# Expert weights in 4 MB transfers, and the order of scatter, gather, last expert and final norm changed

## The reference

```python
gu = xb @ w1[ex] + b1[ex]                 # w1: 1024 x 2048 for each of 32 experts
gate = jnp.minimum(gu[:, :D_FF_EXPERT], SWIGLU_LIMIT)
up = jnp.clip(gu[:, D_FF_EXPERT:], -SWIGLU_LIMIT, SWIGLU_LIMIT)
glu = gate * jax.nn.sigmoid(gate * SWIGLU_ALPHA)
return ((up + 1.0) * glu) @ w2[ex] + b2[ex]   # w2: 1024 x 1024
...
contrib = yb * row_w[:, None]             # weighted by the router's share, summed per token
...
return rmsnorm(x, final_g)
```

## Time and profile before

| | before |
|---|---|
| time, median of 3 runs | 1141.22 us (1140.94 to 1141.25) |
| the profiled execution: its own time | 1141.12 us |
| the profiled execution: its span, first to last instruction | 1139.3 us |
| PE busy | 1078.2 us, 95% of the span |
| DVE busy | 285.8 us, 25% |
| ACT busy | 102.2 us, 9% |
| read from memory | 434.98 MB, 383 GB/s over the span |
| 2 MB transfers | 192, each 40.7 us (median) from issue to landing |

### The profile page before, as it was taken

How to read it: one execution, slowest core, us unless ns; L and a number is a source line. 1 busy time by engine, 2 the same in 40 slices (tenths; PEclk the granted TensorE clock), 3 DMA queues, 4 the chain that set the end, 5 groups by cost and what they waited for, 6 DMA issues and landing times.

```text
span 1139.3 us, 13050 instructions
## 1 busy us (share of the span) xinstructions
PE 1078.2 (95%) x5177; PEld 474.2 (42%) x5177; DVE 285.8 (25%) x614; ACT 102.2 (9%) x215; POOL 11.2 (1%) x20
## 2 busy tenths in 40 slices
PE   7999999899999999999999999999999999999996
PEld 6788788733333333333333333333233323333332
DVE  4652422322222222222222222221211112222222
ACT  1121430200000000000000000000000000000001
POOL 1100000000000000000000000000000000000000
PEclk9999999999999999999999999999999999999999
DMA  9963158589999999999999999999999999999994
GB/s 364 370 258 123 60 224 349 203 350 399 427 429 427 430 427 429 429 427 430 427 430 427 430 427 429 429 427 430 427 429 428 430 427 429 429 427 430 427 430 193
DMA packets 35378, 436.31 MB, mean 383 GB/s; under 512 B 5312, under 2 KB 5696, under 8 KB 7488
## 3 DMA queue, kind: packets, MB, share of 16 engines
q1 hardware_dynamic: 34640, 435.63, 91.3%
q10 hardware_dynamic: 720, 0.42, 0.1%
HBM read 434.98 MB, written 1.05 MB: 383 GB/s over the span
## 4 chain that ended last, share of the span: by engine, by line
PE 71%; DMA 18%; SPq 6%; DVE 4%; issue 1%; ACT 0%; another core or an unknown queue 0%; POOL 0%; DVEq 0%; POOLq 0%; ACTq 0%
PE bank L762 27%; DMA ring<-in_w 17%; PE bank L791 15%; PE bank L490 8%; SPq L342 5%; PE bank L729 4%; PE bank L679 4%; PE bank L685 3%; PE bank L604 2%; PE bank L586 2%; DVE work L1118 1%; PE bank L747 1%; PE bank L525 1%; PE bank L539 1%; DMA ring<-in_w_in 1%; PE bank L510 1%
## 5 line engine op out<-in xcount | busy, mean ns | idle before, releaser
L762 PE MATMUL bank<-ring,work 128*64 128x512 f32 x2048 | 451.1, 593 | 22.6 <-DMA ring<-in_w 21.8
L762 PEld LDWEIGHTS bank<-ring,work 128*64 128x64 f32 x2048 | 144.4, 137 | 309.4 <-issue 259.1
L791 PE MATMUL bank<-ring,work 128*64 128x512 f32 x1024 | 235.5, 602 | 18.1 <-DVE work L1118 18.1
L791 PEld LDWEIGHTS bank<-ring,work 128*64 128x64 f32 x1024 | 68.2, 137 | 142.0 <-issue 116.3
L1109 DVE TENSOR_SCALAR work<-bank 128x512 f32<-128x512 f32 x32 | 22.1, 692 | 418.0 <-PE bank L762 418.0
L490 PE MATMUL bank<-ring 128*128 128x256 f32 x432 | 96.5, 381 | 0.0
L1228 ACT ACTIVATE work<-work 128x512 f32<-128x512 f32 x32 | 20.1, 629 | 758.4 <-DVE work L1109 758.4
L490 PEld LDWEIGHTS bank<-ring 128*128 128x128 f32 x432 | 81.1, 190 | 13.2 <-issue 2.4
L679 PE MATMUL bank<-x2n,work 128*64 128x512 f32 x264 | 63.9, 604 | 0.8 <-DVE work L1024 0.8
L729 PE MATMUL bank<-work 64*128 64x512 f32 x256 | 63.6, 615 | 0.9 <-DVE work L1122 0.9
L1044 DVE TENSOR_TENSOR work<-bank,vec 128x256 f32<-128x256 f32 x66 | 25.0, 420 | 141.2 <-PE bank L685 141.2
(11 more groups left out here) (174 smaller groups left out, 441.6 us busy)
## 6 DMA issues: line engine op xcount, KB each, us to landing
ring<-in_w SPq DMA_DIRECT2D x192, 2048.0 KB, 40.7
ring<-in_w_in SPq DMA_DIRECT2D x16, 1024.0 KB, 17.5
ring<-in_w_out SPq DMA_DIRECT2D x4, 1024.0 KB, 4.7
ring<-in_w_up_a SPq DMA_DIRECT2D x2, 1024.0 KB, 12.2
ring<-in_w_up_b SPq DMA_DIRECT2D x2, 1024.0 KB, 7.6
ring<-in_na_rpb SPq DMA_DIRECT2D x1, 1536.0 KB, 18.4
out<-x2n SPq DMA_DIRECT2D x4, 256.0 KB, 2.1
ring<-in_consts SPq DMA_DIRECT2D x1, 864.0 KB, 13.3
```

The costliest lines, as they stand in the source:

```text
L762: last = pe.matmul(bank[CAP * a:CAP * (a + 1), bk, :], kT, pairs[:, pair_of(par, k // 2), at + q * 512:at + (q + 1) * 512], start=False, s ...
L791: last = pe.matmul(bank[CAP * a:CAP * (a + 1), BH, :], fT, pairs[:, pair_of(par, c), at + a * 512:at + (a + 1) * 512], start=f == 0, stop= ...
```

## The change

It has these parts.

1. Transfers. The weights of the experts are laid out so that two neighbouring chunks form one run of 32 KB per partition. Experts 4 to 29 ("quads") are loaded with three transfers of 4 MB each instead of six of 2 MB, each waiting until PE has used both chunks that it replaces. Experts 0 to 3 and 30 stay at 2 MB. In expert 31 the last w1 chunk comes in two pieces and the last w2 chunk in three.
2. Alignment. Chunk 0 moves to slot 12, chunks 1 to 24 to slots 0 to 11, twice around, and odd experts use pairs 0 to 5 in order. Four of the early 2 MB loads of expert 1 wait for one chunk less than before, and expert 1's second one is issued ahead of the wait for the attention's end.
3. PE's order within an expert. `scatter()` and `gather()` no longer follow the w1 matmuls: the scatter comes at k == 4, the gather at k == 6. After the last w1 matmul the next thing in PE's stream is the wait for `hid_ready`. The wait for `xgT_ready` is split in two halves. In the last expert `turn_gathered` is left out.
4. The b1 split. Its transfers no longer wait for `scale_done`, four of its six steps on DVE move to c == 3, two stay at c == 4. The router's weights are laid out for one contiguous run per partition, and ACT squares x ahead of issuing three small transfers.
5. The final norm. ACT sums the squares in halves of 512, DVE multiplies by final_g meanwhile, and the scaling by the norm's factor is shared by DVE and ACT, each with its own store.

The core of the diff:

```diff
+            def load_quad(blk, q, par, used):
+                w, at = (w1, q) if q < W1_CH // 2 else (w2, 0)
+                first = pair_of(par, 2 * q)
+                sp.wait_ge(chunk_used, used)
+                sp.dma_start(pairs[:, first:first + 2, :].rearrange("p s n -> p (s n)"),
+                             w[bass.ds(blk, 1), at].rearrange("e p n -> p (e n)")).then_inc(quad_landed[par][q], 16)
...
-            with sp.Fori(1, E // 2) as j:
+            with sp.Fori(2, E // 2 - 1) as j:
                 for par in range(2):
-                    for c in range(BLK):
-                        load_chunk(2 * j + par, c, par, (2 * j + par - 2) * BLK + (PRE + c + 1))
+                    for q in range(BLK // 2):
+                        load_quad(2 * j + par, q, par, (2 * j + par - 2) * BLK + (PRE + 2 * q + 2))
...
                 for k in range(D // P):
-                    if k % 2 == 0:
+                    if k % 4 == 0:
+                        pe.wait_ge(xgT_ready, 2 * b + (k // 4 + 1))
+                    if last_one and k // 2 == 3:
+                        pe.wait_ge(piece_landed[k - 6], 16)
+                    elif quads:
+                        if k % 4 == 0:
+                            pe.wait_ge(quad_landed[par][k // 4], landings)
+                    elif k % 2 == 0:
                         pe.wait_ge(pair_landed[par][k // 2], landings)
+                    if k == 4 and not first:
+                        pe.wait_ge(down_ready, b)
+                        scatter()
+                    if k == 6:
+                        pe.wait_ge(pick_ready, b + 2)
+                        gather()
...
-                if not first:
-                    pe.wait_ge(down_ready, b)
-                    scatter()
-                pe.wait_ge(pick_ready, b + 2)
-                gather()
                 pe.wait_ge(hid_ready, b + 1)
                 turn(BH, lambda j: hid[:, j * P:(j + 1) * P], 4, hidT_done)
...
-                    if f == TURN_F:
+                    if f == TURN_F and not last_one:
...
-                if c == 4:
+                if c == 3:
                     dve.wait_ge(b1_landed, 16 * PARTS)
...
+                if c == 4:
                     ch.link(dve.tensor_tensor(b1_raw[low, :], b1_raw[low, :], b1_parts[low, :], ALU.subtract))
...
+                    act.activation(junk[:, 2 * m + a, :], bank[:, BY + 2 * m + a, :], ACT.Square, scale=D ** -0.5,
+                                   accum_out=ssq[:, a, m:m + 1]).then_inc(square_act, 1)
...
+                act.activation(x2n[:, m, 512:D], x2n[:, m, 512:D], ACT.Identity, scale=rstd[:, 2, m:m + 1]).then_inc(act_out, 1)
```

More of the change, by code:

```diff
@@ L245, in build_block @@
         b1_split = sem("b1_split")
-        landed = [sem(f"chunk_landed{n}") for n in range(SLOTS)]
+        landed = [sem(f"chunk_landed{n}") for n in range(SLOTS + 1)]
         pair_landed = [[sem(f"pair_landed{par}_{c}") for c in range(W1_CH + W2_CH)] for par in range(2)]
@@ L269, in build_block @@
         scatT_done, scatT_ready, down_ready, scatter_done = sem("scatT_done"), sem("scatT_ready"), sem("down_ready"), sem("scatter_done")
+        piece_landed = [sem(f"last_piece_landed{n}") for n in range(5)]
+        z_done, square_act, act_out = sem("z_done"), sem("square_act"), sem("act_out")
         y_done, out_ready, out_stored = sem("y_done"), sem("out_ready"), sem("out_stored")
@@ L278, in slot_of @@
         def slot_of(chunk):
-            return chunk % SLOTS
+            return (chunk - 1) % SLOTS if chunk else SLOTS
         def landings(chunk):
-            return 16 * (chunk // SLOTS + 1)
+            return 16 * ((chunk - 1) // SLOTS + 1) if chunk else 16
+        quad_landed = [[sem(f"quad_landed{par}_{q}") for q in range((W1_CH + W2_CH) // 2)] for par in range(2)]
+        LAST_CUTS = {3: [(0, slice(0, 2048)), (1, slice(2048, 4096))],
+                     5: [(2, slice(0, 2048)), (3, slice(2048, 3072)), (4, slice(3072, 4096))]}
         def pair_of(par, c):
-            return (c + 1) % BLK if par else BLK + c
+            return c if par else BLK + c
         BLK = W1_CH + W2_CH
@@ L327, in _ @@
                 sp.dma_start(xT[:, ks, :], xT_in[:, ks, :]).then_inc(xT_landed[n], 16)
-                sp.dma_start(ring[:, 0, cols], w_in[0][:, cols]).then_inc(first_landed[n] if n < 2 else landed[0], 16)
+                sp.dma_start(ring[:, SLOTS, cols], w_in[0][:, cols]).then_inc(first_landed[n] if n < 2 else landed[SLOTS], 16)
             def chunk_source(n):
@@ L382, in _ @@
             load_chunk(0, 5, 0, PRE)
[L383 removed]
+            for par in range(2):
+                for c in range(BLK):
+                    load_chunk(2 + par, c, par, par * BLK + PRE + c + 1)
+            with sp.Fori(2, E // 2 - 1) as j:
                 for par in range(2):
[L385 to L386 removed]
+                    for q in range(BLK // 2):
+                        load_quad(2 * j + par, q, par, (2 * j + par - 2) * BLK + (PRE + 2 * q + 2))
+            for c in range(BLK):
+                load_chunk(E - 2, c, 0, (E - 4) * BLK + PRE + c + 1)
+            for c in range(BLK):
+                if c not in LAST_CUTS:
+                    load_chunk(E - 1, c, 1, (E - 3) * BLK + PRE + c + 1)
+                    continue
+                sp.wait_ge(chunk_used, (E - 3) * BLK + PRE + c + 1)
+                for n, cols in LAST_CUTS[c]:
+                    sp.dma_start(pairs[:, pair_of(1, c), cols], pair_source(E - 1, c, cols)).then_inc(piece_landed[n], 16)
             sp.wait_ge(chunk_used, PRE + (E - 1) * BLK + 1)
@@ L399, in _ @@
             for m in range(MT):
[L400 to L403, removed]
+                sp.wait_ge(out_ready, m + 1)
+                sp.dma_start(out[0, m * P:(m + 1) * P, 0:512], x2n[:, m, 0:512]).then_inc(out_stored, 16)
             sp.wait_ge(out_stored, 2 * 16 * MT)
@@ L436, in project_first @@
             def project_first():
-                w = ring[:, 0, :].rearrange("p (k n) -> p k n", n=CW)
+                w = ring[:, SLOTS, :].rearrange("p (k n) -> p k n", n=CW)
                 for n, ks in enumerate(FIRST):
-                    pe.wait_ge(first_landed[n] if n < 2 else landed[0], 16)
+                    pe.wait_ge(first_landed[n] if n < 2 else landed[SLOTS], 16)
                     for a in range(2):
@@ L807, in _ @@
             expert_block(1, 1, 16)
-            with pe.Fori(1, E // 2) as j:
+            for par in range(2):
+                expert_block(2 + par, par, 32)
+            with pe.Fori(2, E // 2 - 1) as j:
                 for par in range(2):
-                    expert_block(2 * j + par, par, j * 16 + 16)
+                    expert_block(2 * j + par, par, (j - 1) * 16, quads=True)
+            expert_block(E - 2, 0, 48)
+            expert_block(E - 1, 1, 48, last_one=True)
             n_over = pe.value_load(ctrl[0:1, OVER:OVER + 1], min_val=0, max_val=OVER_MAX)
             with pe.If(n_over > 0):
+                pe.wait_ge(xg_ready, E + 1)
+                turn_gathered()
                 with pe.Fori(0, OVER_MAX) as j:
                     with pe.If(j < n_over):
-                        expert_block(j + E, 0, j * 16 + 16 * (E // 2 + 1))
+                        expert_block(j + E, 0, j * 16 + 64)
                     pe.nop()
@@ L1135, in _, with weigh, mean_square, scale_out @@
             dve.wait_ge(final_g_landed, 16)
-            for m in range(MT):
[L1137 to L1144, removed]
+            def weigh(m, a):
+                return dve.tensor_tensor(x2n[:, m, a * 512:(a + 1) * 512], bank[:, BY + 2 * m + a, :],
+                                         gf_b[:, a * 512:(a + 1) * 512], ALU.mult)
+            def mean_square(m):
+                dve.wait_ge(square_act, 2 * m + 2)
+                dve.tensor_scalar(msq[:, 2, m:m + 1], ssq[:, 0, m:m + 1], ssq[:, 1, m:m + 1], EPS,
+                                  ALU.add, ALU.add).then_inc(msq_ready, 1)
+            def scale_out(m):
+                dve.wait_ge(rstd_ready, 3 + m)
+                dve.wait_ge(z_done, 2 * m + 2)
+                dve.tensor_scalar(x2n[:, m, 0:512], x2n[:, m, 0:512], rstd[:, 2, m:m + 1], None,
+                                  ALU.mult).then_inc(out_ready, 1)
+            for m in range(MT):
+                dve.wait_ge(y_done, m + 1)
+                weigh(m, 1).then_inc(z_done, 1)
+                dve.wait_ge(square_act, 2 * m + 1)
+                weigh(m, 0).then_inc(z_done, 1)
+                if m == 0:
+                    mean_square(0)
+            scale_out(0)
+            mean_square(1)
+            scale_out(1)
         @block.scalar
@@ L1150, in _ @@
             act.dma_start(C("ident"), consts[:, CONST["ident"]]).then_inc(ident_landed, 16)
+            for n, ks in enumerate(FIRST):
+                act.wait_ge(xT_landed[n], 16)
+                act.activation(square[:, ks, :], xT[:, ks, :], ACT.Square).then_inc(square_done, 1)
```

(12 more changed lines are left out.)

65 lines of the change are left out of this document (35 added, 30 removed).

## The result

The changed kernel takes 1261.55 us (median of 4 runs, 1259.63 to 1263.71) against 1141.24 before, a ratio of 1.105 (95% interval 1.103 to 1.107). It is slower by 120 us. The prediction had the sign and the order of size, and it named the two things that cost the time.

A forecast was written before the change was run, and what follows sets the result against it. Transfers bound the kernel before, PE after, at 30.06 us per expert. 225.77 + 33.74 + 931.86 less 0.6, + 9.1 + 1.82 gave 1201.7; clock falls of 21.7 made 1223 us, range 1196 to 1257.

The forecast's parts named there:

- What bounds the kernel: Per expert before the change: transfers set the pace at 29.37 us, PE needs 27.15, leaving PE 2.2 us of slack.
- The bare chain: From last w1 matmul to the turns: PE waits uncovered for DVE's hidden values, 2.91 us in every expert.
- the spacing without clock falls: From one expert's b1 product to the next: 27.15 + 2.91 = 30.06 us at the high clock.
- the rival without falls: PE's clock never falls in the expert loop: 1202 us in all, chance 0.11.
- the price of a fall: Low PE clock after the gap before the turns: 0.7 us per expert, bounds 0 and 1.77.
- a full fall in each expert: Each of 31 experts pays 1.77 us for low clock: 1256.6 us or a little more, chance 0.11.
- start of expert 0's w1: Early part up to expert 0's w1: 228.35 less 2.58 for the b1 split's wait, 225.77 us.
- expert 0, to the next b1 product: From expert 0's w1 start to the next b1 product: 1.87 us longer than before, 33.74 us.
- 31 experts, to w2's end: 31 experts of 30.06 us, less 0.6 for the last one's saved turns, plus 21.7 for clock falls.
- end: From w2's end to the span's end: 10.1 us before, some 1.0 less after (bounds 0 and 2), 9.1.
- outside the span: Part of the execution's time not inside the profiled span: 1.82 us, as before the change.
- The rival on the other side: Transfers stay the bound if PE's period is below 29.2 us per expert: faster, about 1135 us, chance 0.06.

The follow-up runs named there:

- a_fill6: Changed kernel plus 6 needless gather-shaped products per expert except the first, between the last w1 matmul and the hid_ready wait: 1206.57 us, ratio 1.058.
- b_order_only: Kernel before the change with only the scatter moved to k == 4 and the gather to k == 6: 1263.6 us, ratio 1.106.
- a_scatter_back: Changed kernel with the scatter alone put back behind the w1 matmuls, the gather still at k == 6: 1142.24 us, ratio 0.9997.

## Why the prediction was right and wrong

**What bounds the kernel.** The reading of the pace held: PE 27.15 by itself, the transfers 29.37, PE the bound after the change. The bare chain was forecast at 2.91, and the wait in it measured at 2.86; the spacing without clock falls was forecast at 30.06 and measured at 30.08 (a_fill6). The forecast of the rival without falls, 1202, stands against 1205.54 for the profiled execution of that kernel; of the difference 2.5 us are in the early part and 0.7 in the end (both below).

**The clock.** This is the step that failed: the price of a fall, taken as 0.7 us per expert between bounds of 0 and 1.77. It measured 1.8 (1.78 against the measured 30.08, 1.80 against 30.06), two and a half times the forecast and at the upper bound. I argued that a low stretch beginning inside the gap spends half of itself on no work, and that not every expert need have one. In the trace each of experts 1 to 31 has one, and they start late: in expert 3 the clock falls as the turns begin, so that a stretch of 3.4 us costs 1.21 to 1.44 and not 0.9. And in each third expert the low stretch is twice as long (6.8 us against 3.4, by the windows above) and costs 2.68. The single fall in the earlier trace rows was the price of one stretch of 3.4 us and no bound on what an expert can lose. What came was my rival "a full fall in each expert", 1256.6 and "a little more if the low level should last longer", to which I had given 0.11.

The range ended at 1257, which is that rival without the little more. With the clock at its bound, it was the early part (3.8 us late in sum) and the end (0.7) that carried the time over the edge.

**The sum, term by term**, against the profiled execution. The forecast sum is 1223.4.

| term | forecast | measured | difference |
|---|---|---|---|
| start of expert 0's w1 | 225.77 | 231.55 | +5.8 |
| expert 0, to the next b1 product | 33.74 | 263.27 - 231.55 = 31.72 | -2.0 |
| 31 experts, to w2's end | 931.3 + 21.7 | 1251.29 - 263.27 = 988.0 | +35.0 |
| end | 9.1 | 1261.1 - 1251.3 = 9.8 | +0.7 |
| outside the span | 1.82 | 1.93 | +0.1 |

Together +39.6, which is 1263.0, the time of that execution. Nearly all is the clock term: 31 x (1.80 - 0.7) = 34.

**The b1 split** was forecast to take away a wait of 2.58 us. It stayed at 2.50, and a new one of 1.64 came. I had counted on DVE's free time at c == 3. That was there, but the data wasn't: the last of its transfers was issued at 10.0 us and DVE had them at 38.4. I had not asked when they land. PE was thus 4.6 us later than forecast at the first gather, which then ran at the low clock in this execution (3.44 us against 1.94), and that makes the 5.8 of the table with 0.3 less of a wait behind it. Expert 0 got back 1.7, as its w2 was not at the low clock this time.

**The 32 KB runs** were forecast at 4.7 us of transfer time and 0 on the path. The first held: 5 us between the two kernels where the transfers are the bound, at 431 GB/s against 428. The second was not run by itself. It fits that PE never waits for a weight transfer in the changed kernel after expert 0, and that b_order_only, without the 32 KB runs, loses as much (ratio 1.106 against 1.105). By the Trainium skill, "DMA: Bandwidth & Descriptors", section "Where 436 GB/s comes from", the ceiling is 435.2; the trace agrees in that no window of 200 us or more comes above 432; single slices of 28 us read up to 437 (page of a_scatter_back). The 2.0 us for each DMA, which the prediction took from the same page of the Trainium skill, stand there for transfers that GpSimd issues, and these are issued by SP: 78 more transfers made 5 us here and not 156.

**The end** won 0.3 us (9.8 against 10.1) and not 1.0. With the squares in halves POOL's first factor comes later, 3.8 us after w2's end against 3.5, and POOL's second factor and the last scaling still follow one another. **Alignment and early loads** were put at 0 and were not run by themselves.

**The rival on the other side** had its point of decision wrong. I set it at a spacing of 29.2 for PE, where transfers and PE balance in the late part. But the loss begins earlier. Before the change 31 experts took 1129.2 - 260.2 = 869 us, 28.03 each, because the first half ran at PE's 27.15 on the lead in the ring. The slack is therefore 0.9 us per expert over the whole run and not 2.2. a_scatter_back shows it: spacing 28.00, PE never starved, and the time of the kernel before. Half of the cover was enough to break even, not to win.

## What to carry to other kernels

Before moving work on an engine that carries out its stream in order, look at what that work covers: here 3.79 us of matmuls hid a chain of 2.9 us on another engine, and moving them left the chain bare in every expert. Count the slack over the whole run, with the lead that the buffers give, and not from the stretch in which the other resource happens to be late. And a repeated gap on PE has a second price, the clock: here it came in every period of the loop, so its price is to be taken at full, with longer falls in the range.

## What the runs showed of the hardware

The clock's falls settle into a pattern. In each of experts 1 to 31 PE has some 4.3 us with nothing but six short turns (2.86 + 0.88 + 0.57, at the high clock). In each of them the granted clock fell from 2.4 to 1.2 GHz, and the spacings repeated as 32.8, 31.5, 31.3 us, in two different kernels (the changed one, and b_order_only). With 2.4 us of the same kind (0.94 + 0.88 + 0.56, a_scatter_back) it did not fall in the loop. In a_fill6, where 0.29 + 0.88 + 0.57 were left, neither. Needless matmuls that end before the wait does bought 55 us.

The length of one gap does not decide by itself. Expert 0 of the changed kernel has the same gap, and its turns and w2 run at the high clock:

```profile
254.18 0.87 PE L711 MATMUL bank<-cst,work 128*128 128x128 f32 x6 [2.93 <-DVE work L1159]
255.62 3.65 PE L829 MATMUL bank<-ring,work 128*64 128x512 f32 x16 [0.57 <-DVE work L1162]
```

In a_fill6, whose expert 0 has the same code and the same wait of 2.93, they take 1.54 and 4.36: the clock fell. And in the kernel before it fell in expert 0 with a gap of 2.5. What decides between them stays open.

The b1 transfers are slow in this kernel. The three of them (32 partitions each, 0.79 MB in all) are in flight in this window of the changed kernel, beside chunks of the projection:

```profile
30.00:34.00 4.00, 4.00 (x20) 3.54 (x19) 0.86 (x2) 0.00 (x0) 4.00 (x5) 1.00 0.98 182
```

The DMA engines are busy (0.98) at 182 GB/s, where 8 KB runs to all 128 partitions move at 424. Whether it is the few partitions that slow them was not tested: the three also read the same rows of memory.
